# Every tile that the matrix engine reads placed at a multiple of 128 bytes, in a two-block fp32 network on one core

## The reference

```python
def first_block(x, ...):
    for l in range(DEPTH):                       # DEPTH = 2
        x = x + token_mixers(rmsnorm(x, mix_norm_g[l]), pos, w_in[l], ..., w_branch[l], w_out[l])
        h = rmsnorm(x, ffn_norm_g[l])
        x = x + (swiglu(h, ffn_w1[0], ffn_w3[0], ffn_w2[0]) if l % 2 == 0
                 else moe_ffn(h, router_w[0], moe_w1[0], moe_w3[0], moe_w2[0]))
    return rmsnorm(x, final_norm_g)

def token_mixers(h, pos, w_in, ..., w_branch, w_out):
    u = h @ w_in                                 # columns of four branches, and gates
    ...                                          # retention, ssd, gla, mlstm: chunked scans
    ybr = jnp.stack([y_ret, y_ssd, y_gla, y_ml], axis=2)
    merged = jnp.sum(jax.nn.sigmoid(mgate) * jnp.einsum('bsnv,nvd->bsnd', ybr, w_branch), axis=2)
    return merged @ w_out

def swiglu(h, w1, w3, w2):                       # D_FF = 2816
    return (jax.nn.silu(h @ w1) * (h @ w3)) @ w2

def second_block(x, c, ...):
    for l in range(DEPTH):
        mod = jax.nn.silu(c) @ ada_w[l] + ada_b[l]
        h = rms_norm(x, g_pre_mix[l]) * (1.0 + scale_m) + shift_m
        ...                                      # attention over 128 keys, causal pools
        x = x + gate_m * rms_norm(mix, g_post_mix[l])
        h = rms_norm(x, g_pre_ffn[l]) * (1.0 + scale_f) + shift_f
        x = x + gate_f * rms_norm((jax.nn.silu(h @ w_gate[l]) * (h @ w_up[l])) @ w_down[l], g_post_ffn[l])
    return x
```

## The kernel before

| tiles | address mod 128 before |
|---|---|
| `x`, `xn`, `hThi`, `hTlo`, `raw`, `whi`, `wlo`, `cst` | 0 |
| `lmask` (8 x 128 bytes, read by VectorE alone) | 64 |
| `cols` 64, `rows_t` 96, `small` 0, `rope_cos`, `rope_sin` | 64 |
| `gate_tanh`, `yhi`, `ylo`, `obuf`, `osq`, `scoresA`, `scoresB`, `rowbuf`, `arena0` | 64 |
| `arena1` | 32 |
| all tiles of the three nets with 256 tokens, `hi_beside`, `lo_beside`, `qraw`, `qrot`, `keys_values`, `utok`, `probT`, `pooled`, `attended`, `mod_sum`, `mod`, `final_gain`, `attention_tables`, `router_tokens` | 64 |
| `idx` (64 bytes) | 64 |
| all that lies behind `idx`: `pick`, `put`, `slots_hi`, `slots_lo`, `outputs_hi`, `outputs_lo`, and the experts' tiles | 0 |

## Time and profile before

### The profile page before, as it was taken

One profiled execution on the slowest core, in us unless ns is written; L12 is line 12 of the kernel. 1 busy time (PEld: TensorE's weight loads), 2 busy tenths in 40 slices (PEclk: granted clock), 3 DMA queues, 4 the chain that ended last, 5 costly groups with the idle time before them and its releaser, 6 DMA issues.

```text
span 2088.1 us, 24723 instructions
## 1 busy us (share of the span) xinstructions
PE 2021.7 (97%) x10190; PEld 1681.7 (81%) x10190; DVE 1647.7 (79%) x1586; ACT 1190.3 (57%) x1267; POOL 63.4 (3%) x93
## 2 busy tenths in 40 slices
PE   7999999999999999999999999999979999899998
PEld 6888788878887778888888888888867787787887
DVE  5778889756878778989899999999886986676454
ACT  6444354446544367777777777777745444445443
POOL 0000010000000000000000000000010000100000
PEclk9999999999999989999999999999999999999999
DMA  8444479855444558999999999999963897534551
GB/s 310 155 175 141 153 273 379 344 196 189 146 162 142 180 217 343 363 376 349 356 362 365 352 358 362 370 364 368 371 226 127 335 380 300 187 137 172 191 181 61
DMA packets 78739, 549.03 MB, mean 263 GB/s; under 512 B 9110, under 2 KB 11030, under 8 KB 12950
## 3 DMA queue, kind: packets, MB, share of 16 engines
q1 hardware_dynamic: 74160, 536.45, 68.5%
q10 hardware_dynamic: 4460, 10.93, 1.5%
HBM read 546.20 MB, written 1.15 MB: 262 GB/s over the span
## 4 chain that ended last, share of the span: by engine, by line
PE 86%; DVE 8%; ACT 2%; POOL 1%; issue 1%; DMA 1%; ACTq 0%; POOLq 0%; DVEq 0%
PE bank L444 82%; PE bank L471 2%; DVE wlo L1125 2%; POOL small L2328 1%; ACT whi L1118 1%; DVE xn L1701 1%; DVE scoresB L1713 1%; DVE gate_tanh L1697 0%; DMA raw<-in_ffn_up 0%; DMA cols<-in_cols 0%; DVE x L2077 0%; DVE xn L2087 0%; PE bank L564 0%; DVE hTlo L1625 0%; PE bank L950 0%
## 5 line engine op out<-in xcount | busy, mean ns | idle before, releaser
L1125 DVE TENSOR_TENSOR wlo<-raw,whi 128x2048 fp32r<-128x2048 f32 x459 | 1046.6, 2285 | 253.7 <-ACT whi L1118 251.6
L1118 ACT ACTIVATE whi<-raw 128x2048 fp32r<-128x2048 f32 x459 | 877.1, 1914 | 364.4 <-PE bank L444 296.7
L444 PE MATMUL bank<-whi,hThi 128*128 128x512 f32 (+1 forms) x1088 | 428.4, 394 | 17.5 <-DVE hTlo L1625 7.9
L444 PE MATMUL bank<-whi,hTlo 128*128 128x512 f32 (+1 forms) x1088 | 419.8, 386 | 0.0
L444 PE MATMUL bank<-wlo,hThi 128*128 128x512 f32 (+1 forms) x1088 | 419.6, 386 | 0.0
L444 PE MATMUL bank<-whi,slots_hi 128*128 128x512 f32 x704 | 274.4, 390 | 0.0
L444 PE MATMUL bank<-whi,slots_lo 128*128 128x512 f32 x704 | 274.3, 390 | 0.0
L444 PE MATMUL bank<-wlo,slots_hi 128*128 128x512 f32 x704 | 274.0, 389 | 0.0
L444 PEld LDWEIGHTS bank<-whi,hThi 128*128 128x128 f32 x1088 | 206.8, 190 | 69.6 <-issue 14.3
L444 PEld LDWEIGHTS bank<-whi,hTlo 128*128 128x128 f32 x1088 | 206.6, 190 | 41.4
L444 PEld LDWEIGHTS bank<-wlo,hThi 128*128 128x128 f32 x1088 | 207.0, 190 | 39.2 <-issue 1.0
(11 more groups left out here) (321 smaller groups left out, 2316.1 us busy)
## 6 DMA issues: line engine op xcount, KB each, us to landing
raw<-in_moe_up SPq DMA_DIRECT2D x176, 1024.0 KB, 7.0
raw<-in_moe_down SPq DMA_DIRECT2D x88, 1024.0 KB, 6.9
raw<-in_w_in SPq DMA_DIRECT2D x72, 1024.0 KB, 4.8
raw<-in_ada_w SPq DMA_DIRECT2D x48, 1024.0 KB, 7.2
raw<-in_second_up SPq DMA_DIRECT2D x44, 1024.0 KB, 4.9
raw<-in_ffn_up SPq DMA_DIRECT2D x22, 1024.0 KB, 5.5
raw<-in_second_down SPq DMA_DIRECT2D x22, 1024.0 KB, 4.8
raw<-in_w_out SPq DMA_DIRECT2D x16, 1024.0 KB, 4.9
```

Of the source, the lines that this page charges most:

```text
L444: m = mm(dst, l_, r_, start=start and i == 0, stop=stop and i == len(pairs) - 1)
L1118: s.then_inc(s.unit.activation(split_slots(p)[0][:, 0:n], slot_of_ring(raw, p, NRAW)[:, 0:n], ACT.Copy), ("hi", p), sem="weights_hi")
L1125: e.then_inc(e.unit.tensor_tensor(lo[:, 0:n], slot_of_ring(raw, p, NRAW)[:, 0:n], hi[:, 0:n].bitcast(F32), ALU.subtract), ("lo", p), sem=sem)
```

## The change

A padding of 64 bytes is put behind the masks, so that `cols` and all that follows moves up by 64 bytes; the slice keeps the tile's size for those who use it. `idx` takes 128 bytes in place of 64, which keeps the experts' tiles at 0. The two arenas are made a little larger, and `carve` rounds each piece up to 32 words (128 bytes). `arena0` already lies behind the padding and comes to 0 with it, and its new size, a multiple of 128 bytes, brings `arena1` to 0. `x` to `cst` stay where they are. `small` goes from 0 to 64, and `rows_t` from 96 to 32. No instruction is added, taken away or moved on any engine, and none changes its size.

```diff
+LINE = 128
 ...
-        lmask = sb(ctx, "lmask", a["lmask"].shape[1], U8)
+        lmask = sb(ctx, "lmask", a["lmask"].shape[1] + LINE // 2, U8)[:, 0:a["lmask"].shape[1]]
 ...
-        arenas = [sb(stage, "arena0", 3092), sb(stage, "arena1", 4626)]
+        arenas = [sb(stage, "arena0", 3136), sb(stage, "arena1", 4640)]
 ...
             for n in sizes:
                 out_.append(arenas[b % 2][:, at:at + n])
-                at += n
+                at += -(-n // (LINE // 4)) * (LINE // 4)
 ...
-        idx = inner.enter_context(nc.sbuf_tensor("idx", [P, NT * NE], mybir.dt.uint32))
+        idx = inner.enter_context(nc.sbuf_tensor("idx", [P, LINE // 4], mybir.dt.uint32))
 ...
-                v.then_inc(vcopy(idf, idx[:, :]))
+                v.then_inc(vcopy(idf, idx[:, 0:NT * NE]))
```

## The result

The changed kernel takes 2106.59 us (median of five runs, 2104.59 to 2108.08), the kernel before 2092.24 us (median of five, 2089.38 to 2097.58). The ratio is 1.0061, with a 95% interval of 1.0047 to 1.0075: slower by 13 us as the ratio has it, 14.4 us between the medians, where 1.4 us less was forecast and the range ended at 2101 us. The profiled execution of the changed kernel took 2104.59 us, its span is 2102.8 us, 14.7 us more than that of before. In the changed kernel's lines every number above 60 is one higher.

What follows compares the result with a forecast made beforehand. TensorE's matmul steps were taken to bound the kernel. Terms 0.7 + 0.2 + 0.2 + 0.3 = 1.4 us less gave 2097.22 - 1.4 = 2095.8 us, shaded to 2095; range 2084 to 2101 us.

Steps and rivals of the forecast that it cites:

- That TensorE's steps are the time: Whole kernel: TensorE has matmuls in flight for 97% of the span, so time is a sum of matmul start-to-start steps.
- Parts 1 to 3: Nets' down products, branch products and weights beside the rings, tiles moved from 64: 0.7, 0.2 and 0.2 us less.
- a delay that is worked off sooner: Runs behind a break: delay gone within some ten steps at 0, later at 64; about 0.02 us per run.
- Part 4: The 1142 shorter matmuls on moved tiles, transposes included: 0.3 us less, range 0 to 2.3.
- the other engines: VectorE and ScalarE steps on moved tiles: change by at most 2 ns each, put at nothing for the end.
- The step that failed: Up products and nearly all of the experts' part: tiles unchanged modulo 128, so no change.
- The slower rival: Every matmul on a moved tile: both operands at 0 hinder each other, 2174 x 6 = 13 us more, 2110 us; chance 0.05.
- The 16-byte lines: Skill's rule for SBUF: penalty per 16-byte line crossing, so 64 is as good as 0; parts 1 to 3 worth 0.
- The two levels of runs: The three runs of the kernel before fall on 2089.8 and on 2097.2 to 2097.6 us; either may be drawn.

Runs made afterwards that it cites:

- experiment 6: Kernel before with the two slot buffer pairs 32 and 192, 96 and 160, or 224 and 16 bytes above the streamed pieces: 2101.58, 2107.88, 2099.07 us.
- experiment 7: Kernel before with `slots_lo` alone apart, by 64 (first pair) and 128 bytes (second): 2105.59 us; with `wlo` alone 128 apart: 2125.84 us.
- experiment 2: Kernel before with `idx` taking 192 bytes in place of 64, so only `pick`, slots and the experts' tiles move, by 128 bytes: 2109.44 us.
- experiment 3: Kernel before with 128 bytes put ahead of `x`, so every tile moves and all distances stay: 2092.76 us.
- experiment 1: Changed kernel with `idx` taking 256 bytes in place of 128, so the experts' tiles lie at 128 modulo 256: 2091.39 us.

## Why the prediction was wrong

*That TensorE's steps are the time* held. The loss is in them; its idle time changed by 0.9 us. One reading under it was wrong and did no harm: I called VectorE and ScalarE similarly busy in the two stretches of rows 9. They are busy 88% and 74% of the time beside the slots, 66% and 46% beside the net's run, and the slots step faster all the same.

*Parts 1 to 3*, the tiles that come from 64 to 0 modulo 128, went as predicted, somewhat better. Tile views of the three nets, first and last of their 88 matmuls with `gatedThi_ffn`; before, then after:

```profile
L444 PE MATMUL bank<-whi,gatedThi_ffn x88: 388/394/498, 311.9 to 469.1; 128*128 128x512 f32 x88
...
L444 PE MATMUL bank<-whi,gatedThi_ffn x88: 392/394/481, 1653.2 to 1808.0; 128*128 128x512 f32 x88
...
L444 PE MATMUL bank<-whi,gatedThi_ffn x88: 392/394/481, 1929.8 to 2080.9; 128*128 128x512 f32 x88
```

```profile
L445 PE MATMUL bank<-whi,gatedThi_ffn x88: 389/389/501, 314.7 to 471.6; 128*128 128x512 f32 x88
...
L445 PE MATMUL bank<-whi,gatedThi_ffn x88: 389/389/481, 1668.8 to 1823.2; 128*128 128x512 f32 x88
...
L445 PE MATMUL bank<-whi,gatedThi_ffn x88: 389/389/481, 1944.9 to 2095.6; 128*128 128x512 f32 x88
```

From first to last, up products in between included, they take 0.3, 0.4 and 0.4 us less, 1.1 in all against the 0.7 forecast (0 to 1.3). The down run that stepped at 228.7 steps at 227.6. How the gain comes about is not as I read it, as a delay that is worked off sooner. Before, the steps of a down run repeat 227, 229, 231 ns to its end, on average over 28 unbroken runs behind transposes; in the changed kernel they settle at 227 after ten.

*Part 4* and the other engines can't be told from no change. The transposes of `gated_ffn` went from 273 to 272 ns, VectorE's product from 417 to 415. Groups by form of the changed kernel:

```profile
L472 PE MATMUL bank<-cst,gated_ffn 128*128 128x128 f32 x132 | 19.8, 272 | 0.0
```

```profile
L1930 DVE TENSOR_TENSOR gated_ffn<-silu_ffn,bank 128x256 f32<-128x256 f32 x44 | 18.0, 415 | 18.7 <-ACT silu_ffn L1395 18.7
```

*The step that failed* stands at the head of the working: the experts' tiles stay where they are modulo 128, and so "the up products, and nearly all of the experts' part, don't change". I took over the change's own measure, the multiple of 128, as the only one. The runs showed in its place that the distance to the streamed tile modulo 256 counts: moved from 0 to 128, it made these matmuls step at 232.6 ns and not 227.0, and the experts' stretch 15.1 us longer. My rows couldn't tell 128 from 256: the cheap stretches (slots, `hThi`) all had both operands at 128 modulo 256, the dear ones had one at 64. "At 0 modulo 128" and "in step with the streamed tile modulo 256" explained them equally well. The addresses were known: the experts' tiles moved by an odd multiple of 128 against rings that stayed. The prediction bounded each moved tile that changed its place modulo 128, and left out of both sum and range 3168 matmuls that moved without changing it. Had I given them the 6 ns that rows 8 show for a dear place, 3168 x 6 = 19 us would have stood as the upper bound.

*The slower rival* spoke of the stationary and the streamed operand beginning at the same place in a block of 128 bytes, and so hindering each other. It was near in its size, 6 ns, and wrong in its sign: tiles at the same place are the cheap ones, and the loss came where a distance of 0 became one of 128. That its 2110 us lies near the measured 2106.6 is luck: it charged 2174 matmuls on tiles that changed their place modulo 128, of which the long ones (nets, branches, weights beside the rings) got faster, and the loss came from 3168 others.

*The 16-byte lines* that I set against the trace (the Trainium skill, "SBUF — State Buffer", Specifications (TRN2)) are not refuted by the 16 bytes of experiment 6, which are free, but 32 bytes, a whole number of such lines, cost 6.5 ns a step. The Trainium skill also says, in "TensorE: Matmul & The Clock Gate", Part 2, that loading the next tile's weights doesn't take read bandwidth from the running matmul. If that is read to mean that the two reads don't affect each other, the runs here disagree: with the same instructions the step grows by 3% (227.0 to 233.5 ns) when only the distance of the two tiles changes, and in experiment 7 a matmul starts 5.8 ns late when nothing but the tile loaded for it is out of place. That it is bandwidth that is lost was not shown.

## What to carry to other kernels

When back-to-back matmuls of TensorE with 512 streamed columns set the time (fp32r, the only type tried here), lay out the stationary and the streamed tiles at the same place modulo 256 bytes, each pair that meets; a common multiple of 128 is not enough, and where the common place lies made no difference (128 and 0 were tried). The matmuls of 256 columns didn't gain by it. A padding moves everything behind it, also what was placed well by chance: list the addresses before and after for each pair of operands, with the count of matmuls. And when a comparison of rows supports a rule about addresses, look for the larger moduli under which the same rows would read the same.

## What was not expected of the hardware

- The cost of a distance is neither smooth nor symmetric: 16 bytes free, 32 to 160 and 224 bytes about 6 to 7 ns on a step of 227, 192 bytes 2 ns. At 256 columns and a distance of 128 there was none.
- Behind most breaks of transposes or 256-column matmuls, the first five to ten steps are slow at distance 0 too, before and after alike. Not behind all: the branch run of the changed kernel that is shown above follows 256-column matmuls and steps at 226.8 ns from its second matmul on. What causes this was not tried.
- The stretch from the start to the first slots, which experiments 2 and 3 leave alone at distances that don't change, ended at 757.9 and 755.0 us against 752.5. The granted clock accounts for nearly all of it. It stands at 0.50, the level of 1.2 GHz, in six stretches ahead of the slots in the profile of experiment 2, 27.3 us in all, in 20.5 us of that of experiment 3, and in 17.1 us of that of the kernel before. If work at that level takes twice as long, 10.2 us more of it cost 5.1 us of the 5.4 in experiment 2, and 3.4 us more cost 1.7 us of the 2.5 in experiment 3 (estimates from the granted clock in these traces). The same stretch in experiment 2 and in the kernel before:

```profile
111.50:114.70 3.20, 3.20 (x9) 2.52 (x8) 2.17 (x7) 2.51 (x3) 0.00 (x0) 0.50 0.35 148
```

```profile
111.50:114.70 3.20, 3.20 (x15) 2.63 (x14) 1.61 (x6) 2.75 (x3) 0.00 (x0) 1.00 0.17 69
```

- The executions of one kernel differ in the same way. Of 23 of the kernel before, those at 2089.7 to 2092.8 us had a mean granted clock of 0.991 to 0.992, those between one of 0.989 to 0.991, and those at 2096.2 to 2097.7 us one of 0.988. The two levels of runs that the prediction spoke of fit this. One profile of each kernel can't resolve differences of a few microseconds of the end; the 757.5 us of the slots, all at a clock of 1.00, repeats within 0.1 us in four kernels.
- The version of experiment 1, with all pairs in step, is the best found: 15 us under the changed kernel. Against the kernel before its ratio of 0.9995 (0.9984 to 1.0006) leaves the expected 1 to 2 us unresolved.
